# A two-block transformer kernel on one core: the weights' three buffers 320 bytes, and everything in the shared region 448 bytes, further along each partition

## The reference

```
x = x + 0.5 * swiglu(rmsnorm(x), ffn1)                  # 1024 -> 2 x 2816 -> 1024
x = x + hybrid_mixer(rmsnorm(x))                        # short conv + gated linear attention, 10 projections
x = x + 0.5 * swiglu(rmsnorm(x), ffn2)
x = rmsnorm(x)
x = x + (neighbourhood attention | retention)(rmsnorm(x)) @ w_out
x = x + square(relu(rmsnorm(x) @ w_up)) @ w_down        # 1024 -> 4096 -> 1024
return rmsnorm(x)
```

## Time and profile before

| | |
|---|---|
| time, median of 3 runs | 1788.98 us (1788.78 to 1790.04) |
| the profiled execution | 1788.58 us |
| its span, first to last instruction | 1786.4 us |
| mean granted clock of TensorE | 0.999 |
| PE busy | 1769.7 us (99%), 10416 matmuls |
| weight loads (PEld) | 1552.9 us (87%) |
| DVE / ACT / POOL busy | 1239.9 (69%) / 846.4 (47%) / 38.2 us (2%) |
| device memory | 170.70 MB read, 97 GB/s over the span |

### The profile page before, as it was taken

The page is one execution under the profiler, slowest core; times in us unless marked ns, Lnnn a source line. Parts: engine busy times, 40 slices in busy tenths (PEclk is TensorE's granted clock), DMA queues, the critical chain, the costliest instruction groups (busy, mean ns, idle before and its releaser), DMA issues.

```text
span 1786.4 us, 26625 instructions
## 1 busy us (share of the span) xinstructions
PE 1769.7 (99%) x10416; PEld 1552.9 (87%) x10416; DVE 1239.9 (69%) x1960; ACT 846.4 (47%) x1444; POOL 38.2 (2%) x38
## 2 busy tenths in 40 slices
PE   9999999999999999999999999999999999999998
PEld 7889989878888889988888998988877788989897
DVE  7948849666676556865695784876677577748474
ACT  6425525444333335643453462554655443627273
POOL 0000000000000000000000000000123000000000
PEclk9999999999999999999999999999999999999999
DMA  5233323332123233333323233334521223233232
GB/s 179 83 106 95 120 88 99 109 103 83 60 83 102 87 103 97 97 118 94 93 84 118 83 109 104 102 100 125 144 69 60 79 89 104 91 99 116 85 119 71
DMA packets 68715, 176.61 MB, mean 99 GB/s; under 512 B 8144, under 2 KB 9424, under 8 KB 68592
## 3 DMA queue, kind: packets, MB, share of 16 engines
q1 hardware_dynamic: 66864, 171.60, 31.1%
q10 hardware_dynamic: 1280, 2.08, 0.3%
q0 software_dynamic: 448, 1.24, 0.3%
HBM read 170.70 MB, written 2.10 MB: 97 GB/s over the span
## 4 chain that ended last, share of the span: by engine, by line
PE 92%; DVE 5%; ACT 2%; issue 2%; DMA 0%; SPq 0%; DVEq 0%; ACTq 0%
PE ps L2012 17%; PE ps L2014 17%; PE ps L2013 17%; PE ps L2097 10%; PE ps L2099 10%; PE ps L2098 10%; PE ps L2034 2%; PE ps L2036 2%; PE ps L2035 2%; DVE wl L1144 1%; DVE wl L1137 0%; PE ps L2376 0%; PE ps L2387 0%; PE ps L2401 0%; PE ps L2246 0%
## 5 line engine op out<-in xcount | busy, mean ns | idle before, releaser
L2012 PE MATMUL ps<-Ahi,wh 128*128 128x512 f32 x920 | 361.8, 393 | 1.6 <-issue 0.7
L2014 PE MATMUL ps<-Ahi,wl 128*128 128x512 f32 x920 | 358.2, 389 | 0.0
L2013 PE MATMUL ps<-Alo,wh 128*128 128x512 f32 x920 | 358.1, 389 | 0.0
L2097 PE MATMUL ps<-BThi,wh 128*128 128x256 f32 x1260 | 353.5, 281 | 2.7 <-ACT tm L566 1.3
L2099 PE MATMUL ps<-BThi,wl 128*128 128x256 f32 x1260 | 351.5, 279 | 0.0
L2098 PE MATMUL ps<-BTlo,wh 128*128 128x256 f32 x1260 | 351.5, 279 | 0.0
L540 ACT ACTIVATE wh<-raw 128x1024 fp32r<-128x1024 f32 (+1 forms) x204 | 211.1, 1036 | 222.2 <-PE ps L2014 189.0
L1137 DVE TENSOR_TENSOR wl<-raw,wh 128x1024 fp32r<-128x1024 f32 (+1 forms) x204 | 245.8, 1206 | 71.7 <-ACT wh L540 69.9
L2097 PEld LDWEIGHTS ps<-BThi,wh 128*128 128x128 f32 x1260 | 236.4, 188 | 4.4 <-DVE BTlo L1209 1.7
L2099 PEld LDWEIGHTS ps<-BThi,wl 128*128 128x128 f32 x1260 | 236.8, 188 | 0.0
L2098 PEld LDWEIGHTS ps<-BTlo,wh 128*128 128x128 f32 x1260 | 235.8, 187 | 0.3
(11 more groups left out here) (331 smaller groups left out, 2684.7 us busy)
## 6 DMA issues: line engine op xcount, KB each, us to landing
raw<-in_w_gu SPq DMA_DIRECT2D x132, 256.0 KB, 2.9
raw<-in_w_d SPq DMA_DIRECT2D x32, 512.0 KB, 3.5
raw<-in_w_dn SPq DMA_DIRECT2D x32, 512.0 KB, 3.9
raw<-in_w_up SPq DMA_DIRECT2D x48, 256.0 KB, 2.8
raw<-in_w_gu SPq DMA_DIRECT2D x20, 512.0 KB, 3.7
raw<-in_w_d SPq DMA_DIRECT2D x16, 384.0 KB, 3.1
raw<-in_w_v SPq DMA_DIRECT2D x8, 512.0 KB, 4.1
raw<-in_w_cc SPq DMA_DIRECT2D x8, 512.0 KB, 3.6
```

The source lines that it names most:

```text
L2012: pe.matmul(ps, wh[:, c], hi[:, k, :], start=(k == 0), stop=False)
L2013: pe.matmul(ps, wh[:, c], lo[:, k, :], start=False, stop=False)
L2014: last = pe.matmul(ps, wl[:, c], hi[:, k, :], start=False, stop=(k == nb - 1))
L2097: pe.matmul(ps, whi[:, w], bhi, start=(new and kp == 0), stop=False, skip_group_check=not new)
```

## The change

The running end is moved by 320 bytes before `raw` is placed, so `raw`, `wh`, `wl` and all that is placed behind them begin 320 bytes later. `M` is moved by another 128, so everything in the shared region begins 448 bytes later. `X`, `Hhi`, `Hlo`, `Ahi`, `Alo`, and what shares the place of the last two, stay. No instruction is added, removed, moved or changed in shape; only start addresses differ.

```
     Ahi, oAhi = sb("Ahi", [P, KT, T], F32R)
     Alo, oAlo = sb("Alo", [P, KT, T], F32R)
+    at[0] += 320
     RAWS, _ = sb("raw", [P, NRAW, 1024])
     WHS, _ = sb("wh", [P, NW, 1024], F32R)
     WLS, _ = sb("wl", [P, NW, 1024], F32R)
...
     small, _ = sb("small", [P, 108])
-    M = (at[0] + 31) // 32 * 32
+    M = (at[0] + 31) // 32 * 32 + 128
 
     VT, _ = sb("VT", [P, 4, D], off=M)
```

## The result

The changed kernel takes 1801.12 us (median of 4 runs, 1799.72 to 1804.53) against 1788.88 us before (1788.25 to 1790.04): a ratio of 1.007, 95% interval 1.0053 to 1.0088. It is slower by some 12 us, where 9 us faster was forecast. The profiled execution took 1800.48 us, its span 1798.4 (before 1786.4).

A forecast was written before the change was run, and what follows sets the result against it. PE was taken to bound the kernel: number of matmuls times their pace, which placement moves by about 2 ns. Terms -8.5 - 1.0 + 0.8 = -8.7 us gave a forecast of 1780 us against 1788.98, range 1766 to 1800.

The forecast's parts named there:

- Term 1: 4248 matmuls streaming `Ahi`, `Alo`, `Hhi`, `Hlo` with 512 columns, distance 0 to 192: -8.5 us, range -8.5 to +9.3.
- Terms 2 and 4: 480 matmuls on 256-column halves of `Ahi`/`Alo`, distance 0 to 192: -1.0 us; 384 in wide units, 0 to 320: +0.8 us.
- Term 3: 4356 matmuls on `BT` and `MT` with 256 columns, distance 320 to 448: taken as 0, bounds -8.7 to +8.7 us.
- Term 5: 192 matmuls streaming `MG`, distance 320 to 448: taken as 0, though a return to 226.8 ns would be -0.4 us.
- Terms 6 and 7: DVE and ACT on the same buffers at new offsets, and DMA into `raw`: cost 0 each.
- No change: Shifts only change which read yields first, or gains and losses cancel: 1789 us, chance 0.22.
- the slower rival: 512-column streams at lines 2012 to 2014 want distance 0, paying 2.2 ns each elsewhere: +9.1 us, 1798; chance 0.33.
- the first number: Time of a down projection of 192 matmuls in the timeline after: forecast 43.15 us, not 43.54.

The follow-up runs named there:

- f2_m192: The kernel before with only the shared region moved, by 192 bytes (distance 0 for what streams from it): 1798.30 us.
- e2_w320: The kernel before with the weights and all behind them 320 bytes further, without the shared region's extra 128: 1811.42 us, ratio 1.0123.
- e1_m128: The kernel before with only the shared region moved, by 128 bytes: 1786.74 us, ratio 0.9987.
- f4_m384: The kernel before with only the shared region moved, by 384 bytes: 1787.00 us.
- h1_w32: The kernel before with the weights and all behind them 32 bytes further: 1810.47 us.
- i1_w32_wo: `h1_w32` plus a wait of PE for its own last matmul ahead of each of the 8 units of `w_o`: 1814.96 us.
- g1_m128_drain: `e1_m128` plus a wait of PE for its own last matmul ahead of the first pair of each run: 1779.24 us, ratio 0.9952.
- h3_after_units: The changed kernel plus a wait of PE for its own last matmul ahead of each unit of the down projections and `w_o`: 1839.82 us.

## Why the prediction was wrong

**Term 1 failed**, and with it sign and range: "I take the saving: 4248 x 2.0 = -8.5 us". It was +27.6 us, 6.5 ns a matmul, three times the upper end of +9.3 us that I had put on it. Two steps of mine led there. The first: I carried a saving from 256 columns to 512. `f2_m192` shows the two shapes side by side at distance 0: the worst pace for 256 columns (120.0) and the best for 512 (226.7). The rival had said so in words, "what suits 256 columns need not suit 512", and I gave it less weight because `MT` at `MG`'s place paid nothing, which is the same mistake again: `MT` streams 256 columns. The second: I took the two distances that showed, 0 and 320, as ends for one that did not. The ends of a pattern sampled at two points bound nothing. The row at distance 192 itself, a stream over the load of `KST` after 0.22 us, which I called no steady stage, misled as well: one spacing of 0.22 us ahead of a matmul of another kind is not a pace.

**Terms 2 and 4** were right in sign: -2.1 us against -1.0 (115.6 ns a matmul), +0.7 against +0.8.

**Term 3** was taken as 0 with -8.7 to +8.7 around it; it came to -13.0 for `BT` and -0.9 for `MT`, past its end. And its mechanism was another: not the distance but which of two paces a run of pairs enters in. The kernel before could have had it as well (the earlier trace rows show 118.0 where 113.3 is to be had).

The gain of the pairs was luck, not foresight: nothing in the sum counted on it. `e2_w320`, whose long runs of pairs stay at 117.8 ns, is 21.5 us slower than the kernel before.

**Term 5** was 0, measured +0.8. **Terms 6 and 7**, DVE, ACT and DMA at nothing, held.

**The rivals.** The slower one named the place (lines 2012 to 2014), the sign and the mechanism, at 1798; the measured 1801 is made of a price three times as high and a gain in the pairs that it did not have, so that its closeness is luck. "No change", the reading by the page "SBUF — State Buffer" of the Trainium skill (section "Who interferes with whom": independent ports, PE waits on no one), is refuted by `e2_w320`: 1.2% by a shift that changes no instruction. Of waiting between engines they show nothing that speaks against the page: DVE's and ACT's durations are unchanged. That the reads of DVE, ACT and DMA leave TensorE's pace alone was not tested.

**The marks.** The down projection at 43.15 us was the mark for right, 43.97 for the slower rival; it read 44.80. "Wrong in its choice if the first number goes up" was the case.

## What to carry to other kernels

When PE is gapless and the count of matmuls is fixed, read its pace from starts, stage by stage: a table of pace against shape and against the distance between the two operands costs nothing. A shift of buffers must be tried for each shape apart, since what is best for one may be worst for the other, and not judged by a gain in one stage. If two stretches with the same shape and placement differ in pace, try one short pause at the entry of the stage before moving any buffer: here 14 pauses brought 0.5% (1779.24 us, faster than both kernels; 1779.71 in the one run with no buffer moved), where the best placement alone gave 0.1% (`e1_m128`). The single 1787.00 us of `f4_m384` lies 0.15 us below the fastest run of the kernel before on record (1787.15), and is no gain that could be told from noise.

## What was not expected of the hardware

- A steady sequence of load and matmul can hold one of two paces at the same clock and the same addresses, 117.8 or 113.3 ns with 256 columns, for over 76 us. It was seen to change only at a stall. Two programs that are alike up to that point took different ones (`h1_w32`, `i1_w32_wo`). The 512-column sequence has two paces at distance 320 (229.0 and 233.3) and at 128 (232.4 and 233.3), and had one at 192, behind 87 pauses.
- The distance between loaded and streaming operand, modulo 256 bytes as far as tried, bears on which paces come up: 226.7 to 233.3 ns with 512 columns, 113.3 to 120.0 with 256. 32 bytes off 0 cost as much as 192.
- A pause for TensorE's own last matmul costs 0.3 us, at distance 0 (`g1_m128_drain`) and at 192 (`h3_after_units`).
- The granted clock can fall to 1.2 GHz for 3.4 us about an idle time of 2.0 to 2.3 us, or stay at 2.4 GHz at the same place of the program: nine of 18 executions have the fall. It costs 1.6 us here, and the page's clock row doesn't show it.

What stays open is why. No run shows what the two reads share, why the pattern has 256 bytes, or what in the entry chooses the pace; nor was every distance tried with 256 columns. That the changed kernel's runs spread more (4.8 us against 1.8) fits a choice made anew in each execution, and the 1.6 us of clock are in such spreads too; only the profiled executions could be read.
